# Three reduced-precision products of split operands for one fp32 product in the gates of a recurrent block

## The reference, cut to what matters

```python
xc = p['conv_b'] + sum(xp[:, k:k + T] * p['conv_w'][k] for k in range(CONV_WIDTH))
xr = xc.reshape(B, T, N_RNN_BLOCKS, RNN_BLOCK)                  # 16 blocks of 64 channels
r = jax.nn.sigmoid(jnp.einsum('btnc,ncd->btnd', xr, p['w_r']).reshape(B, T, D_RNN) + p['b_r'])
i = jax.nn.sigmoid(jnp.einsum('btnc,ncd->btnd', xr, p['w_i']).reshape(B, T, D_RNN) + p['b_i'])
log_a = -RGLRU_C * r.astype(jnp.float32) * jax.nn.softplus(-p['rglru_lambda'].astype(jnp.float32))
a = jnp.exp(log_a)
mult = jnp.sqrt(-jnp.expm1(2.0 * log_a))
b = mult * (i * xc).astype(jnp.float32)
h = linear_scan(a, b, h0.astype(jnp.float32))
y = h.astype(xb.dtype) * jax.nn.gelu(gb)
```

## Time and profile before

| | |
|---|---|
| median of three runs | 2168.73 us |
| span of the profiled execution, first to last instruction | 2158.7 us |
| outside the span, by the median | 10.0 us |
| TensorE busy | 2041.2 us, 95% of the span |
| VectorE, ScalarE, GpSimd busy | 1323.7, 1070.3, 384.8 us |
| stage with the change: eight steps and the last gates | 730.5 to 974.8 us |
| matmul instructions of the gates | 96, 34.3 us busy |

### The profile page before, as it was taken

One profiled execution on the slowest core, in us unless ns is written; L12 is line 12 of the kernel. 1 busy time (PEld: TensorE's weight loads), 2 busy tenths in 40 slices (PEclk: granted clock), 3 DMA queues, 4 the chain that ended last, 5 costly groups with the idle time before them and its releaser, 6 DMA issues. The chain is left out here.

```text
span 2158.7 us, 30487 instructions
## 1 busy us (share of the span) xinstructions
PE 2041.2 (95%) x11897; PEld 1738.4 (81%) x11897; DVE 1323.7 (61%) x1777; ACT 1070.3 (50%) x1402; POOL 384.8 (18%) x282
## 2 busy tenths in 40 slices
PE   5998999999987899999999999899899999999996
PEld 2887777777754799989999999888788888888882
DVE  3623555555564345557344454467799888888885
ACT  3422343443434345665333343221678888778874
POOL 2000011100101121212001001242122222222215
PEclk9999999999999999999999999999899999999998
DMA  7313111113368411115445477433899999999986
GB/s 258 105 62 102 61 48 55 38 57 106 124 206 284 147 42 41 32 48 156 138 138 168 142 216 186 154 118 122 301 373 377 379 378 386 391 385 391 392 327 274
DMA packets 247540, 415.95 MB, mean 193 GB/s; under 512 B 23687, under 2 KB 187271, under 8 KB 221810
## 3 DMA queue, kind: packets, MB, share of 16 engines
q1 hardware_dynamic: 234546, 383.43, 51.5%
q0 software_dynamic: 10944, 24.01, 3.0%
q10 hardware_dynamic: 1920, 6.70, 0.8%
HBM read 382.65 MB, written 45.66 MB: 198 GB/s over the span
## 5 line engine op out<-in xcount | busy, mean ns | idle before, releaser
L418 DVE TENSOR_TENSOR ew_lo<-region,ew_hi 128x2048 fp32r<-128x2048 f32 x192 | 432.4, 2285 | 22.1 <-ACT ew_hi L2216 21.5
L2216 ACT ACTIVATE ew_hi<-region 128x2048 fp32r<-128x2048 f32 x192 | 367.9, 1918 | 112.9 <-DMA region<-in_w 110.3
L418 DVE TENSOR_TENSOR wm_lo<-weights,wm_hi 128x1024 fp32r<-128x1024 f32 x91 | 125.3, 1379 | 143.3 <-ACT wm_hi L1333 142.2
L2736 PE MATMUL PS<-ew_lo,xT_hi 128*128 128x512 f32 x512 | 202.2, 395 | 4.6 <-issue 3.6
L2738 PE MATMUL PS<-ew_hi,xT_hi 128*128 128x512 f32 x512 | 199.7, 390 | 0.0
L2737 PE MATMUL PS<-ew_hi,xT_lo 128*128 128x512 f32 x512 | 199.3, 389 | 0.0
L1488 DVE CUSTOM_DVE_ANT_0 region<-PS,region 128x896 f32<-128x896 f32 (+7 forms) x128 | 91.9, 755 | 144.9 <-PE PS L1739 144.9
L1333 ACT ACTIVATE wm_hi<-weights 128x1024 fp32r<-128x1024 f32 x92 | 97.1, 1057 | 127.4 <-DMA weights<-in_w_pa 67.8
L1211 ACT ACTIVATE region<-region,small 128x896 f32<-128x896 f32 (+7 forms) x128 | 98.8, 772 | 117.5 <-DVE small L1488 117.5
L425 PE MATMUL PS<-h_lo,wx_hi 128*128 128x384 f32 x384 | 133.6, 348 | 3.1 <-POOL wx_lo L418 3.1
L427 PE MATMUL PS<-h_hi,wx_hi 128*128 128x384 f32 x384 | 129.3, 337 | 0.0
(11 more groups left out here) (440 smaller groups left out, 4877.7 us busy)
## 6 DMA issues: line engine op xcount, KB each, us to landing
region<-in_w SPq DMA_DIRECT2D x192, 1024.0 KB, 7.6
weights<-in_w_gate SPq DMA_DIRECT2D x46, 512.0 KB, 3.9
region<-in_w_mod SPq DMA_DIRECT2D x20, 1024.0 KB, 5.3
weights<-in_w_in SPq DMA_DIRECT2D x36, 512.0 KB, 4.0
weights<-in_w_pb SPq DMA_DIRECT2D x24, 512.0 KB, 3.6
weights<-in_w_pa SPq DMA_DIRECT2D x24, 512.0 KB, 3.6
region<-F_d SPq DMA_DIRECT2D x16, 512.0 KB, 6.2
weights<-in_cache_k SPq DMA_DIRECT2D x8, 1024.0 KB, 8.6
```

The costliest lines, as they stand in the source:

```text
L418: return eng.tensor_tensor(lo, x, hi.bitcast(F32), ALU.subtract)
L2216: act(ewh[w], ew[w], ACT.Copy).then_inc(sem(f"eu_hi{w}"), 1)
L2736: mm(out, lh(c), ewl[u][:, c, :], start=first and c == 0, stop=False)
```

## The change

`xc[j]` is split into `xc_hi` (ScalarE, a copy to fp32r) and `xc_lo` (VectorE, the difference), `bw[j]` likewise into `bw_hi`, `bw_lo`. Both pairs of `bw` have two buffers; `xc_hi` and `xc_lo` have one each, in `mixtmp`. TensorE makes three fp32r products for each fp32 product of before.

```diff
+        xch, xcl = part("xc_hi", "mixtmp", 0, TOK), part("xc_lo", "mixtmp", TOK, TOK)
+        bwh, bwl = ([part(f"bw_{n}{j}", "region4", 8192 + 256 * (2 * k + j), 2, P) for j in range(2)] for k, n in enumerate(("hi", "lo")))
...
 ScalarE
+                def split_c(i, j, first=False):
+                    if first:
+                        e.wait_ge(sem("oas_st"), 16)
+                    else:
+                        e.wait_ge(sem(f"ri_done{1 - j}"), i + j)
+                    e.wait_ge(sem(f"bw_in{j}"), i * 64 + 64)
+                    act(bwh[j], bw[j], ACT.Copy).then_inc(sem(f"bw_hi{j}"), 1)
+                    e.wait_ge(sem(f"conv{j}"), i + 1)
+                    act(xch, xc[j], ACT.Copy).then_inc(sem(f"xc_hi{j}"), 1)
...
                         if more:
                             split_x(1, m + 1)
+                        split_c(i, j, old is None)
...
 VectorE
+                def split_c(i, j):
+                    e.wait_ge(sem(f"bw_hi{j}"), i + 1)
+                    lo_of(nc.vector, bwl[j], bw[j], bwh[j]).then_inc(sem(f"bw_lo{j}"), 1)
+                    e.wait_ge(sem(f"xc_hi{j}"), i + 1)
+                    lo_of(nc.vector, xcl, xc[j], xch).then_inc(sem(f"xc_lo{j}"), 1)
...
                 conv(0, 0)
+                split_c(0, 0)
                 with e.Fori(0, CH // 2 - 1) as i:
                     st.base, st.n = i * PER + CONV, 0
                     conv(i, 1)
                     recur(i, 0)
+                    split_c(i, 1)
                     conv(i + 1, 0)
                     recur(i, 1)
+                    split_c(i + 1, 0)
                 st.base, st.n = (CH // 2 - 1) * PER + CONV, 0
                 conv(CH // 2 - 1, 1)
                 recur(CH // 2 - 1, 0)
+                split_c(CH // 2 - 1, 1)
...
 TensorE
                     if n == 0:
-                        e.wait_ge(sem(f"conv{j}"), i + 1)
-                        e.wait_ge(sem(f"bw_in{j}"), i * 64 + 64)
+                        e.wait_ge(sem(f"xc_lo{j}"), i + 1)
                     if n != 1:
                         e.wait_ge(sem("sig"), m * 6 + n)
+                    cols = slice(n * NG, (n + 1) * NG)
                     for k in range(2):
-                        last = mm(PS[:, b + k, 0:NG], bw[j][:, k, :], xc[j][:, n * NG:(n + 1) * NG], start=True, stop=True)
+                        mm(PS[:, b + k, 0:NG], bwh[j][:, k, :], xcl[:, cols], start=True, stop=False)
+                        mm(PS[:, b + k, 0:NG], bwl[j][:, k, :], xch[:, cols], start=False, stop=False)
+                        last = mm(PS[:, b + k, 0:NG], bwh[j][:, k, :], xch[:, cols], start=False, stop=True)
```

## The result

The changed kernel is slower: 2176.66 us (median of 20 runs, 2170.57 to 2182.67) against 2167.89 us (20 runs, 2162.25 to 2179.81) before, ratio 1.0037 with a 95% interval of 1.0026 to 1.0047, so 8.0 us with 5.6 to 10.2 (the two medians alone differ by 8.8 us). A second series of the same kernel gave 1.0051 (1.0032 to 1.0070). The forecast was 2175.2 us, +6.5.

What follows compares the result with a forecast made beforehand. TensorE, 95% busy, was taken to bound the kernel. Steps -1.8, idle +7.3, last round's products -0.8 and clock +1.8 gave +6.5: span 2165.2 plus 10.0 outside, 2175.2 us; 8-in-10 range 2171.0 to 2178.8.

Steps and rivals of the forecast that it cites:

- Price of the products: Gate matmuls: three fp32r products save 0.128 us per fp32 product; groups 0 and 1 gain 0.51, group 2 0.26.
- What of it stays: Seven inner gate rounds: group 2 waits on a panel's DMA, so 0.51 is lost, 0.26 stays; 1.8 us in all.
- Splits beside other work: In the steps, the added ScalarE and VectorE splits cost nothing; VectorE's margin is 1.8 us at worst, 4 otherwise.
- The last round: Chunk 7's gates: TensorE idles 7.3 us (6.8 to 7.8) waiting for VectorE's xc_lo behind recur(3, 0).
- The clock: Behind the last round's idle time TensorE runs at half clock, costing 1.8 us (0 to 2.6).
- Sum in the trace: Whole kernel: steps -1.8, idle +7.3, last round's products -0.8, clock +1.8, total +6.5 us.
- The base: Whole kernel: profiled span of 2158.7 us plus 10.0 us outside it, against the median of 2168.7.
- A: Downstream, at VectorE operations GpSimd stretches: at most 2.4 us given back, total +4.1, 2172.8 us; chance 0.08.
- B: Behind the last round's idle time the clock stays up: total +4.7, 2173.4 us; chance 0.12.
- C: Wait ahead of group 2: steps keep their saving, 3.6 us more, total +2.9, 2171.6 us; chance 0.07.
- D: Every step: VectorE or ScalarE parts come late, 7 us per 1 us over the margin, 2181 or more; chance 0.06.
- E: Gate products: fp32r spaced as fp32 passes, 0.324 us, costing 15.6 us on TensorE, partly hidden; chance 0.02.

Runs made afterwards that it cites:

- e5: Changed kernel with ScalarE's split of the next projection panel moved between the sigmoids of groups 1 and 2 in the inner steps; ratio 0.9991 to the kernel before.
- e7: Kernel before, all products plain fp32, with only ScalarE's panel split moved behind the sigmoids of group 1; ratio 0.9973 to the kernel before.
- e8: Changed kernel with VectorE making the low part of xc twice in every step; ratio 1.0059 to the kernel before.
- e1: Changed kernel with the last chunk, 7, left in plain fp32 products without a split; ratio 1.0010 to the kernel before.
- e2: Changed kernel with all splits and waits kept, but gate products plain fp32 on the unsplit operands; ratio 1.0050 to the kernel before.
- e4: Changed kernel with 32 unused products filling TensorE's wait ahead of the last gate round; ratio 1.0042 to the kernel before.
- c2: Changed kernel measured once more, without edits, as a control; ratio 1.0051 to the kernel before.
- c1: Kernel before measured again, unchanged, as a control; ratio 1.0005 to the kernel before.
- e3: Changed kernel with panel(0) run ahead of all three gate groups of chunk 7; ratio 1.0018 to the kernel before.
- e6: Changed kernel with both the panel split behind the sigmoids of group 1 and chunk 7 in plain fp32; ratio 0.9951 to the kernel before.

## Why the prediction was right, and where its sizes were off

- *Price of the products*: right. 0.177 us against 0.173 for fp32r; groups 0 and 1 gained 0.47 us (0.51 forecast), group 2 0.23 us (0.26).
- *What of it stays*: right, and shown by e5 and e7. TensorE arrived at the last round 1.6 us earlier (968.81 - 774.04 against 966.77 - 770.40), forecast 1.8. The wait ahead of group 2 grew by 3.3 us over seven rounds, forecast 3.6.
- *Splits beside other work*: right. The collision of GpSimd and VectorE came in the steps as the trace before had it; the margin was 2.3 us (1.8 forecast), and e8 used 1.4 us of it without loss.
- *The last round*: 7.08 us against 7.3 from end to start; e1 and e2 show it from both sides.
- *The clock*: fell as forecast. It cost 1.3 us by e4, 1.8 us forecast; by c2's trace it would be 2.1. The rule of the Trainium skill named in the forecast (TensorE: Matmul & The Clock Gate, section "HAM oscillation — how this bites in real kernels"), that work behind a long wait starts at half rate, held in all five profiles with a wait of 5 us or more at this place: the granted clock behind it was 0.50 in each.
- *Sum in the trace*: -1.60 + 7.08 + 0.88 (groups 0 and 1, 3.47 against 2.59) - 0.22 (panel and group 2) = +6.14 us, forecast +6.5. The table has 6.3, since it ends at the start of the last matmul, and behind that start an fp32 matmul needs 0.15 us more than an fp32r one. The wait and the clock were each forecast too long (by 0.2 and 0.5 us), the gains too large (by 0.3 us in all); the errors partly cancel.
- *The base was wrong*: I put 10.0 us outside the span, it is 1.7. The error did no harm by luck: the 10.0 us were the median of before less the span, so adding them only gave that median plus 6.5. Built from the span of 2165.2 with the true 1.7 it would have been 2166.9, 9.8 us too low. The rivals A, B, C, D and E didn't occur.

**Open.** Measured is +8.0 us (5.6 to 10.2), and 11.1 (6.9 to 15.2) the second time; the stretch gives 6.3 and 7.1, both inside the intervals. The surplus over the stretch is positive for every kernel of the table, between 0.2 and 5.1 us, and 1.1 to 1.2 us for the two kernels without splits (c1 and e7). For eight of the eleven the stretch lies inside the interval of the time; for e1, e4 and e8 it lies 0.3 to 0.7 us below it. So part of the surplus may be chance, in the one profile of before that every stretch is measured against and in the timed runs of before, which several experiments share, and a few microseconds may be real and lie in another stage. The longer expert stage doesn't explain it: e2, e3, e5 and e6 have 5.9 to 7.9 us more there than the first profile of before and a surplus of only 0.2 to 1.3 us, and e8, with 2.0 us more there, has the largest surplus, 5.1. Nothing of the change acts in those stages; the cause is not found, and no run isolates it.

## What to carry to other kernels

A faster operation pays only where the work behind it doesn't wait for something else anyway: look for the next wait, follow it to its source (here a DMA ahead of a split ahead of two sigmoids), and move that first; the same edit then made the products worth 0.7 us a round where they had been worth 0.2. Work added beside a busy engine was free in this software pipeline's body, and not in its last round, where no further projection lies between: check the last iteration by itself, and leave it in the old form if that is cheaper. And read a change in the stage where it is made: from one trace to the other, a span of 2160 us differed by more outside that stage than in it.

## What was not expected of the hardware

A VectorE subtraction of 256 elements took 2.62 us beside a GpSimd subtraction, and 0.42 us alone: in all seven rounds it ended 0.28 us behind GpSimd's. A printed idle time in brackets ahead of a matmul is shorter than the loss: ahead of group 2 it says 0.62 us where, by the spacing, 0.8 are lost, with 0.1 of start-up behind; that is why e5 and e7 gained 1.5 and 1.0 us per step and not the 1.3 and 0.8 of the expectations. And the same wait of 6.9 us was followed by half clock over about 3 us in one execution and over more than 4 us in another. The prediction read from one wait of 1.81 us that products behind a shorter wait run near full speed at once; behind e3's wait of 2.0 us, at another place, it fell to 0.50 all the same, though only about 1 us after TensorE had resumed.
